# Routed-expert layer: one-hot "places" of 45 groups compared against key differences that TensorE writes into PSUM

## The reference, cut to what matters

```python
def peer(h, w_q, sub_keys, u_tab, v_tab):
    ...
        expert = jnp.take_along_axis(cand_idx, pos, axis=-1)
        gates = jax.nn.softmax(best, axis=-1).astype(xb.dtype)
        u_sel = u_tab[expert]
        v_sel = v_tab[expert]
        act = jax.nn.gelu(jnp.einsum('td,thkd->thk', xb, u_sel))
        return jnp.einsum('thk,thkd->td', gates * act, v_sel)
```

## Time and profile before

| | us |
|---|---|
| median of 3 runs (2319.29 to 2323.49) | 2321.1 |
| the profiled execution, its own time | 2321.22 |
| its span | 2319.4 |
| u stage ends, choosing begins | 1671 |
| first product of a place | 1716.2 |
| last choose | 1781 |
| value stage begins on PE | 1832.0 |
| last product of the value stage ends | 2308.4 |

### The profile page before, as it was taken

One profiled execution on the slowest core, in us unless ns is written; L12 is line 12 of the kernel. 1 busy time (PEld: TensorE's weight loads), 2 busy tenths in 40 slices (PEclk: granted clock), 3 DMA queues, 4 the chain that ended last, 5 costly groups with the idle time before them and its releaser, 6 DMA issues.

```text
span 2319.4 us, 31507 instructions
## 1 busy us (share of the span) xinstructions
PE 2269.4 (98%) x12458; PEld 2081.4 (90%) x12458; DVE 1754.1 (76%) x3367; ACT 743.2 (32%) x1022; POOL 753.8 (32%) x665
## 2 busy tenths in 40 slices
PE   9999999999999999999999999999987899999997
PEld 7888888889999998998988888888877899999997
DVE  8666777668999898666599997656698866666667
ACT  4345556544335442544111111111375400000001
POOL 0000000000000000000366745555538866566665
PEclk9999999999999999999999999999999999999999
DMA  6554444545854543556799999999932399999998
GB/s 228 186 182 170 170 169 164 186 177 169 246 186 168 177 164 145 182 200 236 256 394 387 413 405 389 373 403 412 351 98 82 136 419 419 418 418 418 417 418 339
DMA packets 112499, 630.28 MB, mean 272 GB/s; under 512 B 14688, under 2 KB 15968, under 8 KB 69984
## 3 DMA queue, kind: packets, MB, share of 16 engines
q1 hardware_dynamic: 53712, 357.92, 40.9%
q0 software_dynamic: 58352, 270.04, 30.2%
q10 hardware_dynamic: 288, 0.31, 0.0%
HBM read 623.95 MB, written 4.26 MB: 271 GB/s over the span
## 4 chain that ended last, share of the span: by engine, by line
PE 91%; DVE 7%; ACT 1%; DMA 1%; issue 0%; POOLq 0%; ACTq 0%; DVEq 0%
PE ps L1159 20%; PE ps L1111 19%; PE ps L801 14%; PE ps L804 7%; PE ps L755 6%; PE ps L778 5%; PE ps L785 5%; PE ps L779 5%; PE ps L1070 4%; DVE ps L2303 3%; DVE work L2343 2%; PE ps L1151 1%; DVE work L2328 1%; PE ps L1082 1%; PE ps L1124 1%
## 5 line engine op out<-in xcount | busy, mean ns | idle before, releaser
L1159 PE MATMUL ps<-weight_raw,pairs 128*128 128x356 f32 x1536 | 462.8, 464 | 2.5 <-DMA weight_raw<-in_peer_v_dense 1.8
L1159 PEld LDWEIGHTS ps<-weight_raw,pairs 128*128 128x128 f32 x1536 | 454.1, 296 | 10.7 <-DMA weight_raw<-in_peer_v_dense 2.3
L1111 PE MATMUL ps<-work,weight_raw 128*128 128x256 f32 x2048 | 442.5, 379 | 0.0
L1111 PEld LDWEIGHTS ps<-work,weight_raw 128*128 128x128 f32 x2048 | 388.9, 190 | 52.7
L2357 DVE SCALAR_TENSOR_TENSOR scan_ws<-work,weight_raw,scan_ws 128x980 f32<-128x980 f32 x253 | 313.7, 1240 | 157.2 <-DMA work<-in_peer_v_rows,weight_raw 142.3
L1790 DVE TENSOR_TENSOR weight_low<-weight_raw,weight_high 128x2048 fp32r<-128x2048 f32 x145 | 332.2, 2291 | 101.9 <-ACT weight_high L1265 101.8
L697 POOL DMA_INDIRECT work<-in_peer_v_rows,weight_raw x255 | 315.6, 1237 | 163.8 <-DVE scan_ws L2357 109.8
L801 PE MATMUL ps<-operand_parts,weight_high 128*128 128x512 f32 x1456 | 354.8, 396 | 3.4 <-DVE slots L1776 1.2
L801 PEld LDWEIGHTS ps<-operand_parts,weight_high 128*128 128x128 f32 x1456 | 268.8, 188 | 61.1 <-issue 7.5
L1265 ACT ACTIVATE weight_high<-weight_raw 128x2048 fp32r<-128x2048 f32 x145 | 276.7, 1908 | 77.6 <-PE ps L804 71.2
L2294 DVE SCALAR_TENSOR_TENSOR work<-work,scan_ws 128x1024 f32<-128x1024 f32 x184 | 220.6, 1225 | 98.8 <-DMA work<-in_peer_u_rows,weight_raw 93.1
(11 more groups left out here) (299 smaller groups left out, 2658.1 us busy)
## 6 DMA issues: line engine op xcount, KB each, us to landing
weight_raw<-in_w_in SPq DMA_DIRECT2D x120, 1024.0 KB, 4.8
weight_raw<-in_peer_v_dense SPq DMA_DIRECT2D x64, 1068.0 KB
weight_raw<-in_peer_u_dense SPq DMA_DIRECT2D x64, 1024.0 KB
weight_raw<-in_w_out SPq DMA_DIRECT2D x32, 1024.0 KB, 4.8
weight_raw<-in_peer_w_q SPq DMA_DIRECT2D x13, 1024.0 KB
weight_raw<-in_conv_w_out SPq DMA_DIRECT2D x8, 1024.0 KB, 5.3
weight_raw<-in_ssm_w_val SPq DMA_DIRECT2D x8, 1024.0 KB
weight_raw<-in_ssm_w_gate SPq DMA_DIRECT2D x8, 1024.0 KB, 4.8
```

The costliest lines, as they stand in the source:

```text
L1111: mm = nc.tensor.matmul(ps[:, 6 + s % 2, h * T:(h + 1) * T], w[:, h, k, :], gained_u[:, k, :], start=(k == 0), stop=(k == KU - 1))
L1159: mm = nc.tensor.matmul(ps_v[:, t, c, :], pairs[:, i // QKEYS, t * P:(t + 1) * P, i % QKEYS], w[:, i % 2, c * CW:(c + 1) * CW], start=(i = ...
```

## The change

Groups P, V and A (45 of the 64 after the change) get their weighted first-key matrix in one DVE operation of 512 elements. For that PE writes the difference "column number minus first key" for 4 tokens into a PSUM bank with one product of 128 rows and 512 columns in bf16 (`edge`), two groups ahead, and DVE compares it with 0 and multiplies by the weight (`scalar_tensor_tensor`).

- `edge_keys` holds the first keys of 4 tokens in 4 rows, rows of ones elsewhere; `edge_tables` holds the column numbers in one row and -1 in the block of each token. POOL writes the ones and the tables (`edges`, after its three prebuilt groups), and four small DMAs bring the keys. Both lie in the memory of value slab 1, which is therefore loaded only when the last group is placed (`pair_done` 64); slab 2 is loaded before it.
- 13 of the 30 groups W become P (`ROLES`), so 17 W, 16 P, 22 V and 9 A.
- Banks: the differences take banks 3 and 5 in the first half and 2, 3, 5 in the second. Choosing has 3 banks in place of 4, the products of the second half 4 in place of 6, and `iota_near` and the turned tiles share bank 4.
- The fifth and sixth spread buffers move; the sixth lies in the memory that `dot_row` reads and is loaded only after the last of those.
- On DVE place(0) stands ahead of choose(37), which before stood ahead of it.

```diff
-ROLES = "WWV" * 8 + "WVAWVVAW" + "WVAWVWAV" * 4
+ROLES = "WPV" * 8 + "WVAPVVAW" + "WVAPVWAV" * 4
...
-PAIR_BANK = [6 + g % 2 if g < DEEP else (6, 7, 0, 1, 2, 3)[(g - DEEP) % 6] for g in range(TT * GROUPS_T)]
+PAIR_BANK = [6 + g % 2 if g < DEEP else (6, 7, 0, 1)[(g - DEEP) % 4] for g in range(TT * GROUPS_T)]
+CHOSEN_BANKS = 3
+EDGE_STEPS = 10
+SLOTS = 4
+EDGED = [g for g in range(TT * GROUPS_T) if ROLE[g] != "W"]
+EDGE_BANK = {g: (3, 5)[n % 2] if g < DEEP else (2, 3, 5)[n % 3] for n, g in enumerate(EDGED)}
+EDGE_AHEAD = 2
...
@@ SP
+                elif b == SPREADS - 1:
+                    sp.wait_ge(row_free[ROW[TT * PICKS - 1]], U_USES[ROW[TT * PICKS - 1]])
...
+            sp.wait_ge(edge_set, 1)
+            for n in range(4):
+                tokens = slice(n % 2 * P // 2, n % 2 * P // 2 + P // 2)
+                sp.dma_start(edge_keys[32 * n + 1:32 * n + 1 + GROUP], d["keys_kept"][0, n // 2, tokens].rearrange("(g a) n -> a g n", a=GROUP)).then_inc(keys_moved, 16)
...
                     sp.wait_ge(hot_ready, CHUNKS_ALL)
-                elif s == RING - 1:
                     sp.wait_ge(w_ready, TT)
-                else:
+                    load_value(2)
+                    sp.wait_ge(pair_done, TT * GROUPS_T)
+                elif s >= RING:
                     sp.wait_ge(v_done, s - RING + 1)
@@ POOL
+            def edges():
+                nc.gpsimd.memset(edge_tables, 0.0).then_inc(edge_set, 1)
+                for n in range(SLOTS):
+                    table = edge_tables[:, n]
...
+                    nc.gpsimd.affine_select(out=table, in_=table, compare_op=ALU.not_equal, fill=-1.0, base=-1 - 32 * n,
+                                            pattern=[[-1, GROUP], [0, P]], channel_multiplier=1).then_inc(edge_set, 1)
...
+                    nc.gpsimd.iota(table[32 * n:32 * n + 1], pattern=[[0, GROUP], [1, P]], base=0, channel_multiplier=0,
+                                   allow_small_or_imprecise_dtypes=True).then_inc(edge_set, 1)
...
+            pool.wait_ge(u_done, PAIR_SLABS)
+            nc.gpsimd.memset(edge_keys, 1.0).then_inc(edge_set, 1)
             for n, g in enumerate(POOLED):
+                if n == PREBUILT:
+                    edges()
@@ PE
-                if g >= 4:
-                    pe.wait_ge(chosen_summed, g - 3)
+                if g >= CHOSEN_BANKS:
+                    pe.wait_ge(chosen_summed, g - CHOSEN_BANKS + 1)
...
+            def edge(g):
+                last = user_before(EDGE_BANK, g)
+                if last is not None:
+                    pe.wait_ge(pair_ready, last + 1)
+                if g >= DEEP:
+                    pe.wait_ge(chosen_summed, TT * GROUPS_T)
+                nc.tensor.matmul(ps[:, EDGE_BANK[g], :], edge_keys[:, g % (GROUPS_T // 2), :],
+                                 edge_tables[:, g // (GROUPS_T // 2)].rearrange("p a n -> p (a n)"), start=True, stop=True).then_inc(edge_done, 1)
...
             def place(g):
+                if g + EDGE_AHEAD in EDGED:
+                    edge(g + EDGE_AHEAD)
                 pe.wait_ge(pair_ready, g + 1)
...
+            pe.wait_ge(keys_moved, 16 * (TT + SLOTS))
+            pe.wait_ge(edge_set, EDGE_STEPS)
+            for g in range(EDGE_AHEAD):
+                edge(g)
             turn_weights(0)
@@ DVE
-                for a in range(GROUP):
-                    tok = GROUP * g + a
-                    ins = v.tensor_scalar(first_hots[FIRST_SLOT[g]][:, a, :], iota_near, first_t[:, tok:tok + 1], weight_t[:, tok:tok + 1], ALU.is_equal, ALU.mult)
                 if ROLE[g] == "V":
-                    plain_hot(hot_at(g), second_t, g).then_inc(pair_ready, 1)
-                else:
-                    ins.then_inc(pair_ready, 1)
+                    plain_hot(hot_at(g), second_t, g)
+                dve.wait_ge(edge_done, EDGED.index(g) + 1)
+                v.scalar_tensor_tensor(out=first_hots[FIRST_SLOT[g]], in0=ps[:, EDGE_BANK[g], :].rearrange("p (a n) -> p a n", a=GROUP), scalar=0.0,
+                                       in1=weight_t[:, GROUP * g:GROUP * (g + 1)].unsqueeze(2).broadcast_to([P, GROUP, P]),
+                                       op0=ALU.is_equal, op1=ALU.mult).then_inc(pair_ready, 1)
```

More of the change, by code:

```diff
@@ L104 @@
 HOT_SLOT = {g: n % 3 if g < DEEP else HOT_RING[(n - SHALLOW) % 5] for n, g in enumerate(ROTATED)}
-BY_GROUP = {"first": dict(enumerate(FIRST_SLOT)), "bank": dict(enumerate(PAIR_BANK)), "hot": HOT_SLOT}
+BY_GROUP = {"first": dict(enumerate(FIRST_SLOT)), "bank": dict(enumerate(PAIR_BANK)), "hot": HOT_SLOT, "edge": EDGE_BANK}
 def user_before(slot_of, g):
@@ L355, in build @@
         first_key, second_key = x_f[:, 3072:3328], x_f[:, 3328:3584]
-        second_half = x_f[:, 3584:3840].bitcast(BF16)[:, 0:TT * PICKS]
+        both_keys = x_f[:, 3072:3584].rearrange("p (c n) -> p c n", c=2)
+        keys_half = x_f[:, 3584:3840].bitcast(BF16).rearrange("p (c n) -> p c n", c=2)
         keep = w_raw[:, NSLAB - 1, :]
@@ L365, in build @@
         v_slabs = [w_flat[:, 2 * CV * n:2 * CV * (n + 1)] for n in range(RING)]
+        edge_keys = w_flat[:, 2 * CV:2 * CV + 1024].bitcast(BF16).rearrange("p (g n) -> p g n", n=P)
+        edge_tables = w_flat[:, 2 * CV + 1024:2 * CV + 2048].bitcast(BF16).rearrange("p (q a n) -> p q a n", q=SLOTS, a=GROUP)
         iota_key = lam_f[:, :, :].rearrange("p a b -> p (a b)")
@@ L370, in build @@
         spread = [scan_ws[:, 2048 + 512 * n:2560 + 512 * n].bitcast(BF16) for n in range(2)] \
-            + [w_flat[:, SPREAD_HOME + 512 * n:SPREAD_HOME + 512 * n + 512].bitcast(BF16) for n in range(SPREADS - 2)]
+            + [w_flat[:, SPREAD_HOME + 512 * n:SPREAD_HOME + 512 * n + 512].bitcast(BF16) for n in range(1, SPREADS - 2)] \
+            + [norm_ws[:, 512:1024].bitcast(BF16)]
         turned_hot = work[:, 4096:6144].rearrange("p (a t n) -> p a t n", a=2, n=P)
@@ L415, in build @@
         ps_turn, ps_keys = ps[:, 4, :], ps[:, 5, :]
-        iota_near = ps[:, 5, 2 * P:3 * P]
+        iota_near = ps[:, 4, 2 * P:3 * P]
         ps_x = ps[:, 6:8, :].rearrange("p c n -> p (c n)")
@@ L437, in build @@
         dve_step = sem("dve_step")
-        bdiag_ready, powers_ready = sem("bdiag_ready"), sem("powers_ready")
+        bdiag_ready = sem("bdiag_ready")
         head_squared, head_summed, qk_ready, v_copied, v_turned, v_ready = (
@@ L1119, in choose @@
                     pe.wait_ge(hot_ready, c + 1)
-                if g >= 4:
-                    pe.wait_ge(chosen_summed, g - 3)
+                if g >= CHOSEN_BANKS:
+                    pe.wait_ge(chosen_summed, g - CHOSEN_BANKS + 1)
                 for a in range(GROUP):
                     tok = GROUP * g + a
-                    mm = nc.tensor.matmul(ps[:, g % 4, a * P:(a + 1) * P], turned_hot[:, c % 2, tok % CHUNK_T, :], pairs[:, :, tok, :],
+                    mm = nc.tensor.matmul(ps[:, g % CHOSEN_BANKS, a * P:(a + 1) * P], turned_hot[:, c % 2, tok % CHUNK_T, :], pairs[:, :, tok, :],
                                           start=True, stop=True)
@@ L1130, in turn_whole @@
                 pe.wait_ge(chosen_summed, GROUPS_T * (t + 1))
-                nc.tensor.transpose(ps_turn[:, t * P:(t + 1) * P], whole_t[:, t * P:(t + 1) * P], ident[:, :]).then_inc(whole_turned, 1)
+                if t > 0:
+                    pe.wait_ge(dots_ready, t)
+                nc.tensor.transpose(ps_turn[:, 0:P], whole_t[:, t * P:(t + 1) * P], ident[:, :]).then_inc(whole_turned, 1)
             def turn_weights(t):
                 pe.wait_ge(w_ready, t + 1)
-                nc.tensor.transpose(ps_turn[:, 2 * P + t * P:2 * P + (t + 1) * P], pick_w[:, t * PICKS:(t + 1) * PICKS], ident[:, :]).then_inc(w_turned, 1)
+                if t > 0:
+                    pe.wait_ge(weights_placed, t)
+                nc.tensor.transpose(ps_turn[:, P:2 * P], pick_w[:, t * PICKS:(t + 1) * PICKS], ident[:, :]).then_inc(w_turned, 1)
+            def edge(g):
[6 more added lines that the diff above has]
+                                 edge_tables[:, g // (GROUPS_T // 2)].rearrange("p a n -> p (a n)"), start=True, stop=True).then_inc(edge_done, 1)
             def place(g):
+                if g + EDGE_AHEAD in EDGED:
+                    edge(g + EDGE_AHEAD)
                 pe.wait_ge(pair_ready, g + 1)
@@ L2310, in sum_dots @@
                 dve.wait_ge(whole_turned, t + 1)
-                v.scalar_tensor_tensor(out=dots[:, cols], in0=ps_turn[:, t * P:(t + 1) * P], scalar=token_rs[:, t:t + 1], in1=dots[:, cols],
+                v.scalar_tensor_tensor(out=dots[:, cols], in0=ps_turn[:, 0:P], scalar=token_rs[:, t:t + 1], in1=dots[:, cols],
                                        op0=ALU.mult, op1=ALU.add).then_inc(dots_ready, 1)
@@ L2464, in _ @@
             weights_out(0)
-            choose(GROUPS_T + AHEAD - 1)
             for g in range(GROUPS_T):
@@ L2475, in _ @@
                 place(g)
-                if g > 0 and g - 1 + AHEAD < GROUPS_T:
+                if g - 1 + AHEAD < GROUPS_T:
```

(2 more changed lines are left out.)

24 lines of the change are left out of this document (15 added, 9 removed).

## The result

The changed kernel took **2305.9 us** (median of 4 runs, 2304.6 to 2308.5) against 2320.6 for the kernel before beside it: a ratio of 0.9929, with a 95% interval of 0.9913 to 0.9945. The forecast was 2307.6, with a range of 2301 to 2316. The profiled execution took 2308.49 us, its span 2306.7, 12.7 less than the 2319.4 of before.

What follows compares the result with a forecast made beforehand. Bounds taken: DMA and PE together in the value stage, a loop through PE and DVE in placing's first half, DVE in its second. Sum: 2321.2 - 4.6 - 3.0 - 0.6 - 6.4 + 1.0 = 2307.6 us, range 2301 to 2316.

Steps and rivals of the forecast that it cites:

- Sizes of the two new instructions: DVE's new operation takes 0.63 us (range 0.60 to 1.13), PE's difference product 0.23 (other end 0.89).
- Start of placing: First places up to V of group 5: PE starts sooner and keeps its pace, -4.6 us (-2.6 if not).
- 1.5 is nearer to 1.01: Start of placing: PE's idle 1.5 us keeps full pace, as 1.01 did and 3.61 did not; hence -4.6.
- Rounds: First half of placing, groups 5 to 26: seven rounds of 6.55 us in place of 6.97, -3.0 us.
- The gathers: POOL's value gathers in the first half: PE's wait of 2.31 us falls to 1.8, -0.6 us.
- Second half: Placing after V 26: DVE no longer the bound, PE becomes it with POOL close behind, -6.4 us.
- Slab 1: Value slab 1, loaded at the end of placing, costs DMA time: 0 to 2.6 us, taken as +1.0.
- the same, but less of it: Rival: smaller gain from lost clock, unchanged gathers, dearer slab and PE/POOL waits: 2313.3 us, chance 0.20.
- More of it: Rival: DVE's second choose wait goes and the slab is free, 2304 us; without PE/POOL restarts 2302; chance 0.09.
- The two slow rivals: New operation takes 1.13 us: 2319.7, chance 0.06; difference product takes 0.89 us: 2330, chance 0.05.

Runs made afterwards that it cites:

- c2: The changed kernel with choose(37) ahead of place(0) on DVE again: 2313.1 us, ratio 0.9965.
- b1: The changed kernel with every difference product issued twice into the same bank: 2315.1 us, ratio 0.9964.
- b2: The changed kernel with every difference product issued four times into the same bank: 2328.0 us, ratio 1.0033.
- a3: The kernel before, with only value slab 2 loaded ahead of slab 1 and slab 1 when the last group is placed: 2323.3 us, ratio 1.0010.
- d0: The changed kernel itself, run again unchanged: 2308.6 us, ratio 0.9945.
- a1: The changed kernel with 12 of the 13 groups that became P back at role W: 2309.3 us, ratio 0.9953.
- d2: The changed kernel with value slab 1 loaded when the last difference product is done: 2309.9 us, ratio 0.9945.
- b3: The changed kernel with DVE's new operation of 512 elements split into four of 128: 2314.4 us, ratio 0.9962.
- a2: The kernel before with the new roles and nothing else: 2327.0 us, ratio 1.0031.
- c1: The changed kernel with POOL's three value gathers issued after its third group in place of its eighth: 2305.3 us, ratio 0.9942.

## Why the prediction was right

- **Sizes of the two new instructions.** Taken 0.63 and 0.23 us apart, measured 0.60 and 0.22. They were taken for 45 groups where there are 47, which changes no term. The nearest rows (the earlier trace rows for the rate of the operation, for the product) were the right ones. The ends of both ranges (1.13 and 0.89) are out. The rule of the Trainium skill (Vector Engine (DVE) Microarchitecture Reference, Points that are easy to get wrong) on a half throughput was set against rows 11, where two sources in SBUF showed none. The new operation, with one source in PSUM, lies outside its words and showed none either: 686 ns, as the 683 of the plain one.
- **Start of placing**, -4.6, measured -4.4. PE stood 1.31 us where 1.5 was worked out, and the pace held. In c2's trace, with 2.38 us of standing, it did not, so the question of the clock belongs in this term; but the last section has longer idle times that left the pace whole, so "1.5 is nearer to 1.01" was not a safe ground for it.
- **Rounds**, 6.55, measured 6.51. The step that two thirds of DVE's saving shorten the loop was right (0.46 of 0.67). b1 and b2 show the other half of it: of the two differences in a round one is on the path and one lies in PE's wait.
- **The gathers**, forecast -0.6, came out at +0.6 in the profiled execution: the stretch exceeds seven steady rounds by 3.1 us in place of 2.6. The step that failed is the one that read a shorter wait as time gained. The wait fell by 0.3 where 0.5 was forecast, and the stretch grew all the same. The clock does not explain it: the slow pace has 16 records in both traces, and in two traces without it (a3, with the old operations, and d0) the excess is 1.3 and 1.5 us, so like against like the term is +0.2 or +0.6. (A gain, of 1.1, comes out only where d0, without the slow pace, is set against the trace of before, with it.) What is left is that PE had 1.01 us of waiting ahead of each V in which to catch up and now has 0.33; that fits, and no run tests it alone.
- **Second half**, -6.4, measured -6.2. PE and POOL are the bounds as forecast: a1 shows POOL (with four more W there it takes 2.5 us longer), b1 shows PE (0.17 for each product more).
- **Slab 1**, forecast +1.0, measured 0 in the change, a3 and d0. The step that failed is the one that turned bytes into time. The bytes left for the stage over 418 GB/s were read as a second bound. But d2 moved a slab's bytes forward for nothing, and every trace without an early wait for a slab has 459.8 to 460.2 us from the first tile to the end of the last wait, whatever went before. PE sets this length, but for the last wait of 1.7 to 2.1 us: in the change 1530 of the stage's some 1620 records start 0.30 us after the one before. This error (1.0) and that of the gathers (1.2) nearly cancelled, which is luck.
- **Where the total came out.** The first slab product was forecast near 1817.4 and came at 1819.95: 1.2 us from a later start of choosing, 0.9 from rounds and gathers, 0.4 from the rest. The value stage and its end gave back 1.6. The profiled execution lies 0.9 us above the forecast and the median 1.7 below, less than the same code differs by; so the total bears out the forecast no more closely than to some 3 us, and the stretches bear out its terms.

Of the rivals, "the same, but less of it" came nearest on the gathers (as before, where they came out 0.6 worse), and its other prices did not come. "More of it" put the slab at nothing, as it is, and expected DVE's second wait of a round to go; it is 0.23 us. The two slow rivals needed 1.13 us an operation or 0.62 us a product; neither came near.

## What to carry to other kernels

Work that moves from a full engine to another pays only where the receiving engine has time: the same roles cost 3.6 us before the differences took DVE off the path and brought 3.1 after. When a loop runs through two engines, count what each saved instruction leaves as latency, and double the cheap instruction in an experiment: it tells in one run which of its places lie on the path. Before a change is judged by 2 or 3 us, run it again unchanged; here the start of placing, the second half and the value stage agreed to 0.1 us between two traces of the same code, while the medians moved by 2.7 and the rounds in between by 1.6, with the clock.

## What was not expected of the hardware

**PE's pace after an idle time is not decided by its length alone.** The slow records are at the lower of the two clocks (1.2 in place of 2.4 GHz): the profile of before grants 0.52 of full speed for 1716.2 to 1719.6, in which PE, after 3.61 us of idling, ran 16 records at about half the pace. Idle times of 1.31 to 1.50 us at the start of placing led to no such records (eight traces). Behind the gathers 2.01 us did in the change and in d2 and not in c2, and 2.02 did not in d0; 2.31 did before and not in a3; 1.85 did in b3. Ahead of the last 48 records of the value stage 1.83 us did in the trace of before (16.43 us) and not in that of a2 (14.73). Early in that stage 2.37 us did in c2 (clock 0.56 for the next 3 us), while c1's 3.24 us did not: the 360 records behind it, shown above, go 0.30 us apart at a clock of 1.00. And in a3 slow records (0.62 from 1789.5 to 1793.2) stand behind waits of only 1.0 us, which before has as well and without them. One fall costs 1.5 to 1.7 us of PE's time. The Trainium skill (TensorE: Matmul & The Clock Gate, What's actually happening) has the half rate as the default that activity lifts; the direction agrees, while the outcome at idle times of 1.0 to 3.2 us differed between traces.

**Stages that an edit does not touch move the total by several us.** The last row product of the u stage ended between 1670.5 and 1681.5 in the fourteen traces, and in the two latest (1677.8 in c2, 1681.5 in a3) PE stood for about 6 us in choosing, 3 to 4 us after it had begun; DVE waits for gathered rows just before (3.39 and 2.64 us in a3). In b1 and b3 the cause is another: PE waited for 2.6 and 2.4 us in all at 1180 to 1187, ahead of the u stage, and some of its records there took over 600 ns where they take 379 (granted clock 0.66 and 0.84 from 1181 to 1186.5), so the u stage began 4 us later (1233 in place of 1229). What held PE up there was not looked into.
